# Prompt attention: in each job's step ScalarE copies the turned probabilities first and takes the coming exponentials after them

## What is computed

```python
def selected_branch(qg, pos_q, kv_g, idx, valid, slopes):
    ...
    s = jnp.einsum('bqgrd,bqgmd->bqgrm', qg, k).astype(jnp.float32) * ATTN_SCALE
    s = s - slopes[:, :, None] * dist[:, :, :, None, :]
    p = masked_softmax(s, mask[:, :, :, None, :])
    return jnp.einsum('bqgrm,bqgmd->bqgrd', p.astype(v.dtype), v)

def window_branch(qg, pos_q, kv_w, pos_k, slopes):
    ...
    p = masked_softmax(s, mask[None, :, None, None, :])
    return jnp.einsum('bqgrk,bkgd->bqgrd', p.astype(kv_w.dtype), kv_w[:, :, 1])
```

## Time and profile before

| | |
|---|---|
| median of 3 executions | 2026.33 us (2026.32 to 2027.14) |
| the profiled execution | 2023.28 us, its span 2021.5 us |
| busy, share of the span | PE 98%, PEld 87%, DVE 63%, ACT 37%, POOL 16% |
| prompt attention, first score to last turn and product | 154.6 to 425.1 us of the span |

### The profile page before, as it was taken

The page is one execution under the profiler, slowest core; times in us unless marked ns, Lnnn a source line. Parts: engine busy times, 40 slices in busy tenths (PEclk is TensorE's granted clock), DMA queues, the critical chain, the costliest instruction groups (busy, mean ns, idle before and its releaser), DMA issues.

```text
span 2021.5 us, 35967 instructions
## 1 busy us (share of the span) xinstructions
PE 1982.9 (98%) x14875; PEld 1756.5 (87%) x14875; DVE 1282.4 (63%) x2190; ACT 741.5 (37%) x1410; POOL 320.2 (16%) x405
## 2 busy tenths in 40 slices
PE   8999999999999999999999999999999999999998
PEld 8897777769679999998999987898888888888896
DVE  3147777656632676676413337768888888888867
ACT  3227777754322545553212021122222222222223
POOL 0030000011400322321000000021222111232206
PEclk9999999999999999999999999999999999999999
DMA  9423010247652222222111222121112111111112
GB/s 232 131 78 112 12 53 2 95 165 248 248 179 56 51 64 61 60 66 80 42 43 52 78 91 78 36 74 42 53 42 72 44 42 42 53 42 60 45 43 84
DMA packets 140750, 159.25 MB, mean 79 GB/s; under 512 B 25842, under 2 KB 122443, under 8 KB 135724
## 3 DMA queue, kind: packets, MB, share of 16 engines
q1 hardware_dynamic: 132556, 114.18, 18.6%
q0 software_dynamic: 8032, 42.78, 6.8%
HBM read 141.36 MB, written 19.76 MB: 80 GB/s over the span
## 4 chain that ended last, share of the span: by engine, by line
PE 90%; DVE 6%; ACT 2%; issue 1%; DMA 0%; POOL 0%; DVEq 0%; SPq 0%; POOLq 0%; ACTq 0%
PE PS L1041 53%; PE PS L1834 12%; PE PS L1311 3%; PE PS L1291 3%; PE PS L1400 3%; PE PS L1729 2%; PE PS L1257 1%; PE PS L1385 1%; PE PS L1259 1%; DVE arena L3057 1%; PE PS L1638 1%; PE PS L1820 1%; PE PS L1320 1%; PE PS L1513 1%; DVE arena L2744 0%
## 5 line engine op out<-in xcount | busy, mean ns | idle before, releaser
L1041 PE MATMUL PS<-x_low,w_high_mlp 128*128 128x344 f32 x1056 | 337.8, 320 | 0.0
L3057 DVE TENSOR_TENSOR arena<-arena,PS 128x512 f32<-128x512 f32 x336 | 224.7, 686 | 95.8 <-PE PS L1834 89.4
L1041 PE MATMUL PS<-x_high,w_low 128*128 128x344 f32 x768 | 246.2, 321 | 0.0
L1041 PE MATMUL PS<-x_high,w_high_mlp 128*128 128x344 f32 x720 | 231.3, 321 | 0.0
L1041 PEld LDWEIGHTS PS<-x_low,w_high_mlp 128*128 128x128 f32 x1056 | 198.2, 188 | 3.0
L1041 PE MATMUL PS<-x_low,w_high_hgrn 128*128 128x344 f32 x600 | 191.9, 320 | 0.0
L2202 ACT ACTIVATE aT<-PS 128x344 f32<-128x344 f32 x90 | 41.0, 455 | 372.2 <-PE PS L1041 313.3
L1834 PE MATMUL PS<-w_down_parts_high,hidden_parts_high 128*128 128x512 f32 x392 | 155.8, 397 | 0.9
L1834 PE MATMUL PS<-w_down_parts_high,hidden_parts_low 128*128 128x512 f32 x392 | 154.1, 393 | 0.0
L1041 PE MATMUL PS<-x_high_a,w_low 128*128 128x344 f32 x480 | 153.5, 320 | 0.0
L1041 PE MATMUL PS<-x_high_b,w_low 128*128 128x344 f32 x468 | 149.6, 320 | 0.0
(11 more groups left out here) (509 smaller groups left out, 4904.6 us busy)
## 6 DMA issues: line engine op xcount, KB each, us to landing
wring<-in_w_in SPq DMA_DIRECT2D x100, 256.0 KB, 3.3
wring<-in_w_up SPq DMA_DIRECT2D x64, 256.0 KB, 3.2
arena<-in_w_down SPq DMA_DIRECT2D x16, 1024.0 KB, 4.9
arena<-in_x_prompt SPq DMA_DIRECT2D x16, 512.0 KB, 3.7
x_high_kept<-x_high_att SPq DMA_DIRECT2D x1, 4128.0 KB, 13.1
arena<-in_w_out SPq DMA_DIRECT2D x2, 2048.0 KB, 7.7
out<-in_cache_win_kv SPq DMA_DIRECT2D x1, 4088.0 KB
out<-arena SPq DMA_DIRECT2D x7, 512.0 KB
```

The lines of the kernel that those rows point to most:

```text
L1041: mm = pe.matmul(out, w, x, start=(start and k == 0 and i == 0), stop=(stop and k == tiles - 1 and i == 2))
L3057: ins = dve.tensor_tensor(y, y, sums, ALU.subtract if m == 4 else ALU.add)
```

## The change

In each step the copy of the first turned group stands ahead of the exponentials on ACT, where it stood behind them. No instruction is added or removed, and no wait: what each instruction waits for stays with it.

```diff
             for j in range(NJ):
-                for x in range(scored(j - 2) + 1 if j else scored(-1), scored(j - 1) + 1):
-                    exp(x)
                 act.wait_ge(t_ps, first_group[j] + 1)
                 if j >= 3:
                     act.wait_ge(pv_ps, (j - 3) // 2 + 1)
                 n = P * len(groups(j)[0])
                 act.activation(PT[j % 3][:, 0, 0:n], PS[:, 4 + first_group[j] % 2, 0:n], ACT.Copy).then_inc(t_act, 1)
+                for x in range(scored(j - 2) + 1 if j else scored(-1), scored(j - 1) + 1):
+                    exp(x)
                 if j % 4 == 1 and j >= 5:
                     parts(j // 4 - 1)
```

## The result

The changed kernel takes **2085.76 us** (median of 4, 2083.16 to 2093.19) against 2026.32 us before (median of 4 on the same chip): ratio 1.0301, 95% interval 1.0281 to 1.0320. The prediction was 2082.4, its range 2071 to 2094.

What follows compares the result with a forecast made beforehand. PE, busy for 98% of the span, was taken to bound the kernel. Terms 52.7 + 2.4 + 1 = +56.1 us on 2023.28 gave 2079.4, and with the median 3.05 above that execution 2082.4 us; range 2071 to 2094.

Steps and rivals of the forecast that it cites:

- Sum: Attention stage: odd two-bank, even two-bank and one-bank terms, 52.7 + 2.4 + 1 = +56.1 us.
- odd steps of the forecast: 32 odd two-bank steps: PE's scores newly wait 1.30 to 1.92 us each for the later exponential, +52.7 us.
- PE's delays count in full: Attention stage: PE goes from turn to scores without a gap, so every delay lengthens the stage, +56 us.
- The room that the busy share of weight loads seemed to leave: Attention stage: by a Trainium skill rule, 61.5 us of PE room would swallow the sum, +0.
- Step 25, the pattern: Odd two-bank example: scores start at 205.91 in place of 204.21, a new wait of 1.70 us.
- Even steps: Even two-bank steps: `pv` behind the turns covers ACT except in the first three per pair, +2.4 us.
- Step 24: Even two-bank example: scores possible at 202.43, and they start at 202.48 before the change, so no wait.
- One-bank steps: Exponential is for a job three ahead, so hardly a wait; bounds -5.8 and +12, taken as +1 us.
- The rival that hides the delay: Attention stage: delayed scores are caught up before the next odd step; 2026.3 us, chance 0.04.
- the one that wins: Attention stage: earlier copy frees `pv` and turns, exponential not late; 2020.5 us, chance 0.03.
- The clock: Attention stage: new PE pauses bring the granted clock to 1.2 GHz; +65 more, 2147 us, chance 0.04.
- The row that I held against it: First 10 us: PE busy for only 4.57 at granted clock 1.00, cited against pauses lowering the clock.

Runs made afterwards that it cites:

- The odd steps run alone: Copy ahead of the exponentials in the odd two-bank steps only, order of before elsewhere: 2081.84 us, ratio 1.0273 against the kernel before.
- +2.66 alone: Copy ahead of the exponentials in the even two-bank steps only, order of before elsewhere: 2029.81 us, ratio 1.0018 against the kernel before.
- +1.66 alone: Copy ahead of the exponentials in the one-bank steps only, order of before elsewhere: 2028.47 us, ratio 1.0009 against the kernel before.
- the other one: Profiled execution from running the changed kernel once more, unaltered; that run measured 2086.73 us, ratio 1.0307 against the kernel before.
- the wait alone: Kernel before, exponential still ahead of copy, but ACT's wait for the turned group moved ahead of both: 2066.85 us, ratio 1.0200.
- With 2.08 us: Changed kernel plus one 256-column copy on ACT ahead of the copy in odd two-bank steps: 2113.26 us, ratio 1.0417 against the kernel before.

## Why the prediction was right

- **Sum.** +56.1 us was forecast for the stage, which "should be about 326 us long": it is 326.71, +56.26. From the first load of one job's turn to that of the next job's, in the two timelines, the gain is 52.2 us in the odd steps of the forecast, 2.45 in the even and 1.6 in the one-bank steps, against 52.7, 2.4 and 1. So the sum is not met by errors that cancel.
- **PE's delays count in full.** Its scores wait 52.6 us longer for exponentials than before, and 3.8 longer where the profile names no releaser (6.7 in place of 2.9), 56.4 together, for a stage that is 56.26 longer. The room that the busy share of weight loads seemed to leave was none.
- **Odd steps.** The odd steps run alone gave 55.07, in a stage at a clock of 0.99. The reckoning took 0.48 us from the copy's start to the next operation, read off a copy followed by another copy. With the change an exponential follows, and in 62 of the 71 two-bank steps in which one does it starts 0.49 after the copy. Step 25, the pattern, is one of the other nine, at 0.62 (216.49 to 217.11), and so waits 1.80 in place of 1.70. The same step of the fourth pair, with the same kind of exponential:

```profile
462.66 0.60 ACT L1974 ACTIVATE arena<-PS 128x512 f32<-128x512 f32 x1 [1.62 <-PE PS L1291]
...
463.15 0.79 ACT L1951 ACTIVATE arena<-PS,arena 128x640 f32<-128x640 f32 x1
```

- **The ninth odd step.** The forecast counts eight odd two-bank steps for a pair of heads and leaves out the ninth, j % 32 = 31. It gained 2.1 us in the three pairs that have another behind them, and the step after it gave as much back: there `pv` had waited 2.0 us in all for DVE's copies before, and no longer does. Leaving it out was right for the sum, but no reason for it was given.
- **Even steps.** +2.4 forecast, +2.66 alone. Step 24 was to come out without a wait and waited for 0.09: it too is one of the nine.
- **One-bank steps.** +1 forecast, +1.66 alone. The mechanism (`turn_parts` waiting for L1959) is there, 4.2 us in 11 waits.
- **The rival that hides the delay** is out, and with it the one that wins: PE's scores wait 55.7 us.
- **The clock** was given 0.04 as a case of its own, +65. It came true on a small scale, together with the forecast: not in the profiled execution of the change, whose stage had a granted clock of 1.00, but in the other one, at 0.98, for 6.1 us more. Of the first four executions, the two at mean clocks of 0.998 and 0.999 took 2083.3 and 2083.2 us, within 1 us of the forecast, and those at 0.994 and 0.993 took 2088.3 and 2093.2; the median, 3.4 us over the forecast, lies between the two groups. That the profiled execution is within 1 us of the median's forecast is luck in part: for an execution like the one profiled before the sum gave 2079.4, and the other 3.8 us are those lost ahead of the stage, where the clock was 0.98. The row that I held against it, PE busy for 4.57 of the first 10 us at a clock of 1.00, did not carry over to the pauses of this stage. The Trainium skill (TensorE: Matmul & The Clock Gate, A second HAM failure mode: psum-queue depth-cycling) tells of a kernel in which frequent short idle times between groups of matmuls made the clock swing; the rows at 0.66 and 0.83 above agree, as far as they show a clock below 1.00 in a stage with such pauses.

## What to carry to other kernels

On an engine that works in order, an operation that waits for the engine next door should stand behind whatever that engine will ask for next. The copy was needed late and the exponential early; putting the copy first made ACT wait first and work afterwards, and two engines that had overlapped took turns. Before moving something ahead, count for each step what the other engine has left in its queue: here one order and the same work cost 0.1 us where a `pv` followed and 1.8 us where none did.

## What the runs showed that was not expected

- **The same operation behind the same copy can start at two distances.** Behind a 512-column copy on ACT the exponential starts 0.49 us after the copy's start in most steps and 0.62 after it in nine. Steps 25 and 121 have the same forms and differ in this (0.62 and 0.49), so what the exponential reads does not explain it. The cause is open.
- **PE's longer pauses go with a lower clock.** With waits of 1.18 us in the odd steps (the wait alone) the stage ran at a granted clock of 1.00 and four executions lay within 1.6 us. With 1.80 us it was 1.00 in one profile and 0.98 in another, and 0.99 with the odd steps alone. With 2.08 us it was 0.92, and PE was busy for some 27 us more. That the pauses bring the clock down is the likely reading and not shown: each of these is one profile, they come from more than one chip, a lower clock also came ahead of the stage (0.98 in the profile of the change), and what exactly makes it fall was not tried apart.
